# Gating tables made and applied ahead of the up tiles, not in a stage of their own

## The reference

```python
# peer(h, w_q, subkeys, u, v), per token; 8 heads, 16 experts each
# scores against two sets of 128 sub-keys, top 16 of each, top 16 of the sums
# -> per token 128 pairs (i1, i2) and gates g (softmax over a head's 16)
# hidden[e] = gelu(h . u[e])       for the experts picked, e = 128*i1 + i2
# y         = sum over picked e of  g * hidden[e] * v[e]
x = x + (g2[:, None, :] * y)
```

## Time and profile before

| | |
|---|---|
| median of 3 runs | 2908.99 us (2905.86 to 2910.26) |
| the profiled execution | 2908.07 us, span 2905.8 us from first to last instruction |
| mean granted TensorE clock | 0.983 |
| TensorE busy | 2771.0 us, 95% of the span |
| DVE, ACT, POOL busy | 1946.6, 1486.4, 1447.3 us |
| last up column to first down matmul | layer 0: 660.50 to 758.68 us; layer 1: 1711.12 to 1808.33 us |

### The profile page before, as it was taken

How to read it: one execution, slowest core, us unless ns; L and a number is a source line. 1 busy time by engine, 2 the same in 40 slices (tenths; PEclk the granted TensorE clock), 3 DMA queues, 4 the chain that set the end, 5 groups by cost and what they waited for, 6 DMA issues and landing times.

```text
span 2905.8 us, 53264 instructions
## 1 busy us (share of the span) xinstructions
PE 2771.0 (95%) x16662; PEld 2418.7 (83%) x16662; DVE 1946.6 (67%) x3521; ACT 1486.4 (51%) x2901; POOL 1447.3 (50%) x1137
## 2 busy tenths in 40 slices
PE   6999999997999999899999988999998999999998
PEld 6689999997777887789999986787878998876666
DVE  7736982338788887758940358888876544477776
ACT  1115554449645555455555568555545643255553
POOL 4831998888554441005989887544430000234442
PEclk8999999999999999899999999999999999999999
DMA  7634556770466663234555730766654533389994
GB/s 255 211 111 143 183 181 241 258 256 12 145 246 224 234 234 120 73 127 151 182 182 189 256 130 36 256 241 219 228 183 138 182 131 122 115 295 358 357 358 181
DMA packets 172454, 562.50 MB, mean 194 GB/s; under 512 B 15521, under 2 KB 18337, under 8 KB 172209
## 3 DMA queue, kind: packets, MB, share of 16 engines
q1 hardware_dynamic: 169968, 556.86, 54.6%
q10 hardware_dynamic: 2368, 4.19, 0.4%
HBM read 559.94 MB, written 1.05 MB: 193 GB/s over the span
## 4 chain that ended last, share of the span: by engine, by line
PE 59%; issue 19%; POOL 10%; ACT 7%; DVE 3%; DMA 1%; POOLq 0%; ACTq 0%; DVEq 0%; SPq 0%
PE bank L1094 20%; PE bank L1124 10%; PE bank L828 7%; PE bank L1417 6%; PE bank L887 5%; PE bank L1438 4%; ACT hT L1670 4%; POOL w_parts L2846 3%; ACT hT L1666 1%; POOL mean L2911 1%; POOL hT L2911 1%; DMA ring<-stream 1%; POOL mean L2913 1%; POOL hT L2913 1%; ACT h_parts L1678 1%
## 5 line engine op out<-in xcount | busy, mean ns | idle before, releaser
L2846 POOL TENSOR_TENSOR w_parts<-ring,w_parts 128x512 fp32r<-128x512 f32 x512 | 661.1, 1307 | 411.3 <-ACT w_parts L1630 378.2
L1094 PE MATMUL bank<-h_parts,w_parts 128*128 128x256 f32 x6144 | 751.8, 284 | 8.4 <-POOL w_parts L2846 6.1
L1094 PEld LDWEIGHTS bank<-h_parts,w_parts 128*128 128x128 f32 x6144 | 743.2, 192 | 9.4 <-issue 4.8
L1630 ACT ACTIVATE w_parts<-ring 128x512 fp32r<-128x512 f32 x512 | 320.0, 631 | 346.3 <-PE bank L1094 283.4
L1124 PE MATMUL bank<-h_parts,a_parts 128*128 128x512 f32 x1536 | 366.4, 394 | 8.1 <-DVE a_parts L2436 8.1
L1124 PE MATMUL bank<-w_parts,a_parts 128*128 128x512 f32 x1536 | 372.1, 398 | 1.3 <-DVE a_parts L2436 1.2
L1124 PEld LDWEIGHTS bank<-h_parts,a_parts 128*128 128x128 f32 x1536 | 284.6, 188 | 83.7 <-DVE a_parts L2436 25.3
L1124 PEld LDWEIGHTS bank<-w_parts,a_parts 128*128 128x128 f32 x1536 | 286.1, 190 | 62.4 <-DVE a_parts L2436 3.5
L1695 ACT ACTIVATE a_parts<-arena 128x256 fp32r (+1 forms) x256 | 107.0, 418 | 367.0 <-PE bank L1124 365.1
L828 PE MATMUL bank<-h_parts,w_parts 128*128 128x256 f32 x2304 | 282.5, 285 | 4.1 <-DVE w_parts L2027 4.1
L828 PEld LDWEIGHTS bank<-h_parts,w_parts 128*128 128x128 f32 x2304 | 279.7, 193 | 5.1 <-issue 4.4
(11 more groups left out here) (401 smaller groups left out, 4528.2 us busy)
## 6 DMA issues: line engine op xcount, KB each, us to landing
ring<-stream SPq DMA_DIRECT2D x594, 512.0 KB, 3.3
arena<-stream SPq DMA_DIRECT2D x105, 1024.0 KB, 7.3
arena<-stream SPq DMA_DIRECT2D x144, 512.0 KB, 4.5
hT<-stream SPq DMA_DIRECT2D x80, 512.0 KB, 4.4
mean<-stream SPq DMA_DIRECT2D x32, 512.0 KB, 4.5
arena<-consts ACTq DMA_DIRECT2D x1, 1536.0 KB, 6.5
xT<-xin ACTq DMA_DIRECT2D x1, 1024.0 KB, 10.7
out<-hT SPq DMA_DIRECT2D x4, 256.0 KB, 2.2
```

The costliest lines, as they stand in the source:

```text
L1094: mm = pe.matmul(bank[k][:, 0:T], w[:, wp, ws], h_parts[:, hp, 4 * j + q, :], start=(j == 0 and q == 0 and i == 0), stop=(j == 1 and q == ...
L1630: act.activation(w_parts[half % HALVES][:, 0, :], ring[slot_][:, j * 512:(j + 1) * 512], ACT.Copy).then_inc(sem(f"{n}_high"), 1)
L2846: pool.tensor_tensor(w[:, 1, :], ring[(base + k) % RING][:, j * 512:(j + 1) * 512], w[:, 0, :].bitcast(F32), ALU.subtract).then_inc(sem(f" ...
```

## The change

There is no table stage. A table group is four tokens, 64 groups in all, and group g is handled with up tile 64 + g (`TABLE_TILE` = 64). In order, for each step:

- DVE makes the four rows of `hot1` by one TENSOR_SCALAR per token (compare `iota`, copied to PSUM bank 6, with the first index, multiply by the gate; both are scalars per partition read from `route`), and `hot2` of the group by one TENSOR_TENSOR. `hot1` lies in the upper half of `hT`, `hot2` in `a_parts`, two groups each.
- TensorE runs the four table matmuls into bank 4 or 5 before the tile's 24 matmuls.
- DVE multiplies the table of group g-1 into all of `W` for its four tokens. For tiles whose gelu isn't there yet `W` holds ones, written by ACT (32 tiles, in its up tiles 56 to 63) and by a DVE memset (32 tiles).
- ACT's gelu of tiles 64 to 127 writes back into the tile's own bank, and DVE multiplies the bank into `W` (`gate_tile`), two steps later. TensorE writes the bank again when that is done.
- The modulation rows are summed by the same steps: one of the eight instructions after each `hot1` row. SP loads a row in two halves of 256 KB, each behind the ring load of one tile.

ACT's and POOL's parts of the one-hot work go away. Layer 0 has modulation rows in all 64 steps, layer 1 in its last 32.

```diff
+GROUP = 4
+GROUPS = T // GROUP
+TABLE_TILE = NK - GROUPS
...
+        hot1 = hT[:, 4:8, :].rearrange("p s (k n) -> p (s k) n", k=2)
+        hot2 = a_parts[:, :, :, :].rearrange("p x a t -> p (x a t)").rearrange("p (s n) -> p s n", n=P)
...
+                with sp.Fori(0, UP_ROWS // 2 - 1) as it:
+                    for k in range(4):
+                        r, i = k // 2, k % 2
+                        slots(it, RING + k, RING + k + 1)
+                        sp.wait_ge(sem("up_made" if i else "up_half"), it * 2 + (done + 2 + r))
+                        sp.dma_start(up_buffer(i), stream[it * 6 + (row + 3 * (2 + r)), :, i * 512:(i + 1) * 512])\
+                          .then_inc(up_landed[i], 16)
...
                 for c in range(RING):
                     sp.wait_ge(sem(f"{n}_low"), 2 * (NK - RING + c + 1))
-                    if c == RING - 1:
-
-                        sp.wait_ge(sem(f"{n}_table_free"), GROUPS + T // 4)
-                    v_load(c)
+                    v_load(c, False)
+                sp.wait_ge(sem(f"{n}_applied"), GROUPS + 2)
+                mod_load(seg, seg[0])
...
+            up_pe(pe, l, ROUTE_TILE, TABLE_TILE)
...
+            pe.sem_inc(sem(f"{n}_tabled"), 2)
+            for half in range(2):
+                first = TABLE_TILE + NK // 4 * half
+                up_pe(pe, l, first, first + NK // 4, rows=(first - UP_FROM[l]) // (2 * UP_ROWS) if first >= UP_FROM[l] else None,
+                      tables=GROUPS // 2 * half)
...
+        def table_pe(pe, n, it, k, first):
+
+            pe.wait_ge(sem(f"{n}_hots"), it * 4 + (first + k + 1))
+            pe.wait_ge(sem(f"{n}_applied"), it * 4 + (first + k + 1))
+            for s in range(GROUP):
+                slot_ = GROUP * (k % 2) + s
+                mm = pe.matmul(bank[4 + k % 2][:, s * P:(s + 1) * P], hot2[:, slot_, :].bitcast(F32), hot1[:, slot_, :],
+                               start=True, stop=True)
+            mm.then_inc(sem(f"{n}_tabled"), 1)
...
                 for k in range(4):
+                    if tables is not None:
+                        table_pe(pe, n, it, k, tables)
+                        pe.wait_ge(sem(f"{n}_gated_tile"), it * 4 + (tables + k + 1))
...
             for b in range(4, 8):
-
+                if b == 7:
+                    pe.wait_ge(sem("up_rows"), l + 1)
...
+            for i in range(ROUTE_TILE, TABLE_TILE):
+                gelu(slice(i, i + 1), i % 4, 2 * (i + 1))
+                if i == ROUTE_TILE:
+                    act.wait_ge(sem("turned"), TT * (l + 1))
+                at = TABLE_TILE + 4 * (i - ROUTE_TILE)
+                act.activation(W[:, at:at + 4, :].rearrange("p i (h n) -> p (i h) n", n=P), ones.unsqueeze(1).broadcast_to([P, 8, P]),
+                               ACT.Copy).then_inc(sem(f"{n}_ones"), 1)
+                high((i + 3) % 8, 2 * (i + 3), tile_at(i + 3), base)
+            with act.Fori(TABLE_TILE // 8, NK // 8 - 1) as it:
+                for k in range(8):
+                    gelu(None, k % 4, it * 16 + 2 * (k + 1), bank[k % 4][:, 0:T])
...
-                    act.wait_ge(sem(f"{n}_table_free"), GROUPS + T // 4)
+                    act.wait_ge(sem(f"{n}_applied"), GROUPS + 2)
+                if k == 1:
+                    act.wait_ge(sem(f"{n}_gated_tile"), GROUPS + 4)
...
+            iota_p = bank[6][:, T:T + P]
+            dve.tensor_copy(iota_p, iota).then_inc(signal("dve_step"), 1)
+            dve.memset(W[:, TABLE_TILE + NK // 4:NK, :], 1.0).then_inc(signal("dve_step"), 1)
...
+            def make_hots(first, it, k, tokens):
+
+                at = it * 16 + GROUP * (first + k)
+                if tokens[0] == 0:
+                    dve.wait_ge(sem(f"{n}_tabled"), it * 4 + (first + k + 1))
+                for s in tokens:
+                    dve.tensor_scalar(hot1[:, GROUP * (k % 2) + s, :], iota_p, route[:, 0, bass.ds(at + s, 1)],
+                                      route[:, 2, bass.ds(at + s, 1)], ALU.is_equal, ALU.mult)
+                    row_step(first, it, k, s)
...
+            def apply_table(first, it, k):
+
+                dve.wait_ge(sem(f"{n}_tabled"), it * 4 + (first + k + 3))
+                dve.wait_ge(sem(f"{n}_gated_tile"), it * 4 + (first + k + 3))
+                part = W[:, :, bass.ds(it * 16 + GROUP * (first + k), GROUP)]
+                dve.tensor_tensor(part, part, bank[4 + k % 2][:, :].rearrange("p (t i) -> p i t", t=GROUP), ALU.mult)\
+                   .then_inc(sem(f"{n}_applied"), 1)
+
+            def gate_tile(first, it, k, last=0):
+
+                dve.wait_ge(sem(f"{n}_applied"), it * 4 + (first + k + 4 - last))
+                dve.wait_ge(sem(f"{n}_gelu"), it * 4 + (TABLE_TILE + first + k + 1))
+                part = W[:, bass.ds(it * 4 + (TABLE_TILE + first + k), 1), :].rearrange("p i t -> p (i t)")
+                dve.tensor_tensor(part, part, bank[k % 4][:, 0:T], ALU.mult).then_inc(sem(f"{n}_gated_tile"), 1)
+
+            def step(first, it, k, skip=False):
+
+                make_hots(first, it, k, (0, 1))
+                if skip and k == 1:
+                    dve.wait_ge(sem(f"{n}_ones"), TABLE_TILE - ROUTE_TILE)
+                if not skip or k >= 1:
+                    apply_table(first, it, k - 1)
+                make_hots(first, it, k, (2, 3))
+                finish_hots(first, it, k)
+                if not skip or k >= 2:
+                    gate_tile(first, it, k - 2)
...
-            pool.wait_ge(sem(f"{n}_route"), TT)
-
-            with pool.Fori(0, T // TURN) as it:
```

More of the change, by code:

```diff
@@ L1079, in peer_pe, with up_pe @@
             back_pe(pe, n, "kv" if l == 0 else "mid", {0: ((act_y, 1), (dve_y, 1)), 2: ((act_y, 2), (dve_y, 2))})
-        def up_pe(pe, l, first, last, rows=None):
+        def table_pe(pe, n, it, k, first):
[6 more added lines that the diff above has]
+            mm.then_inc(sem(f"{n}_tabled"), 1)
+        def up_pe(pe, l, first, last, rows=None, tables=None):
             n = f"p{l}"
@@ L1631, in high, with gelu @@
                                    ACT.Copy).then_inc(sem(f"{n}_high"), 1)
-            def gelu(i, k, count):
+            def gelu(i, k, count, out=None):
                 act.wait_ge(sem(f"{n}_half_free"), HALVES + count)
-                act.activation(W[:, i, :], bank[k][:, 0:T], ACT.Gelu).then_inc(sem(f"{n}_gelu"), 1)
+                act.activation(W[:, i, :] if out is None else out, bank[k][:, 0:T], ACT.Gelu).then_inc(sem(f"{n}_gelu"), 1)
             def tile_at(i):
@@ L1647, in peer_act @@
             high(2, 4, tile_at(2), base)
-            for first, last in ((0, ROUTE_TILE), (ROUTE_TILE, NK - 8)):
-                if first:
-                    act.wait_ge(sem(f"{n}_picked"), TT)
-                with act.Fori(first // 8, last // 8) as it:
-                    for k in range(8):
-                        gelu(bass.ds(it * 8 + k, 1), k % 4, it * 16 + 2 * (k + 1))
-                        high((k + 3) % 8, it * 16 + 2 * (k + 3), it * 32 + tile_at(k + 3), base)
+            with act.Fori(0, ROUTE_TILE // 8) as it:
+                for k in range(8):
+                    gelu(bass.ds(it * 8 + k, 1), k % 4, it * 16 + 2 * (k + 1))
+                    high((k + 3) % 8, it * 16 + 2 * (k + 3), it * 32 + tile_at(k + 3), base)
@@ new lines, in up_row_dve @@
+            r = row % 2
+            total = bank[6][:, r * P:(r + 1) * P]
+            at = lambda n, per: it * (2 * per) + ((done + row) * per + n)
+            w = up_buffer(j // 4)[:, j % 4 * P:(j % 4 + 1) * P]
+            if j % 4 == 0:
+                dve.wait_ge(up_landed[j // 4], at(16, 16))
+            if j == 0:
+                dve.tensor_scalar(total, w, c[:, 0:1], None, ALU.mult).then_inc(sem("up_step"), 1)
+                return
+            if j == 4:
+                dve.wait_ge(sem("up_half"), at(1, 1))
+            else:
+                dve.wait_ge(sem("up_step"), at(j if j < 4 else j - 1, 6))
@@ L2260, in up_mods_dve, with up_rows_dve @@
+            if j == 7:
+                dve.wait_ge(sem("up_column"), at(1, 1))
+            out = up_part(r) if j == 7 else total
+            dve.scalar_tensor_tensor(out, w, c[:, j:j + 1], total, ALU.mult, ALU.add)\
+               .then_inc(sem({3: "up_half", 7: "up_made"}.get(j, "up_step")), 1)
+        def up_rows_dve(dve, l):
             dve.wait_ge(sem("up_column"), UP_DONE[l + 1] + 2)
             for n, (lo, hi) in enumerate(MODS_UP[l]):
-                dve.tensor_tensor(modv[:, lo:hi], bank[7][:, UP_ROWS * n:UP_ROWS * (n + 1)], V("mod_b")[:, lo:hi], ALU.add)\
-                   .then_inc(signal("dve_step"), 1)
@@ L2264, in up_mods_dve @@
[L2264 removed]
+                ins = dve.tensor_tensor(modv[:, lo:hi], bank[7][:, UP_ROWS * n:UP_ROWS * (n + 1)], V("mod_b")[:, lo:hi], ALU.add)
+            ins.then_inc(sem("up_rows"), 1)
+            dve.wait_ge(sem("up_rows"), l + 1)
         def peer_dve(dve, l):
@@ new lines, in peer_dve @@
+            for k in range(4):
+                step(0, 0, k, True)
```

(9 more changed lines are left out.)

176 lines of the change are left out of this document (35 added, 141 removed).

## The result

The changed kernel takes 2831.49 us (median of 4 runs, 2830.2 to 2835.67) against 2907.43 us: ratio 0.9741, 95% interval 0.9724 to 0.9758, some 76 us less. A second set of 5 runs gave 2831.4 us and 0.9737 (0.9715 to 0.9759). The forecast was 2851 us with a range of 2828 to 2889: the direction and the mechanism hold, but the gain was put at 57.6 us and is 76. The profiled execution has a span of 2828.1 us, 77.7 less than before's.

The account below looks back on a forecast made before the run. One-hot making bound the table stage, TensorE the stages around it. 96 x 4.06 + 32 x 3.85 + 2 x 4.5 - 2 = 520.0 us replaces 577.6, 57.6 less: 2851 us, range 2828 to 2889.

Parts of the forecast that it names:

- The stage was bound by making one-hots, and TensorE waited in it: Gating-table stage before down, 98.2 and 97.2 us: ACT and DVE busy 96 to 98% making one-hot rows, TensorE 78%.
- A group of table matmuls, 0.97 us: TensorE's cost for four tokens' table matmuls between up tiles, taken as 0.97 us between 0.89 and 1.13.
- A plain step: An up tile with its table group but no modulation row: 2.88 + 0.97 = 3.85 us, for 32 steps.
- The 0.1 us for what three near bounds cost each other: Added to TensorE's 3.96 us because DVE and the hand-off are close: 4.06 us per step with a modulation row.
- DVE's step, 3.73 us (3.60 to 3.85): DVE's start-to-start sum in a step with a modulation row; stays below TensorE's 3.96 us by 0.2 us.
- the second pointer: Second pointer scalar in DVE's one-hot row operations: costs 0 to 61 ns, so 0.29 us taken per row.
- POOL doesn't slow the steps: POOL's weight splitting beside DVE's new operations: nothing charged, as all but the memset have an input in PSUM.
- the ends: After each layer's last up tile, until the first down matmul: 4.5 us per layer.
- The clock credit of 2 us: Start of down: low clock after the stage with TensorE 78% busy costs 2.4 + 1.6 us; half credited.
- ACT's ones, DVE's memset, SP's half rows at nothing: Side work in and ahead of the up tiles: hidden or done in time, so no time charged.
- the one in which everything fits under TensorE: Rival: steps of 3.88 and 3.77 us, group at 0.89, clock stays high (4 us credit): 2829 us; chance 0.11.
- DVE-bound steps: Rival: DVE overhead makes the 96 steps with a modulation row 4.35 us, 27.8 us less: 2881 us; chance 0.25.

## Why the prediction was right, and where it was off

- **The stage was bound by making one-hots, and TensorE waited in it.** Right: TensorE's own need there was 55 of 91 us per layer, and most of the rest is the gain. Half its matmuls left out of the old stage gained nothing, though at a lower clock.
- **A group of table matmuls, 0.97 us.** Mis-sized: 0.83 and 0.90 in turn; what a group adds to a plain tile is 3.76 - 2.88 = 0.88, the lower bound of 0.89 from the weight loads. The 0.141 per record of the old stage had waits in it. A plain step came to 3.76 us against 3.85: 32 x 0.09 = 2.9 us.
- **The 0.1 us for what three near bounds cost each other.** This is the term that failed. Nothing of it was found: the step is 3.885 us, TensorE's own sum, with DVE at 3.83 beside it, and taking 0.5 us off DVE's part shortens it by less than 0.01. The allowance makes 9.6 us; with the cheaper group the 96 steps differ by 96 x 0.175 = 16.8 us.
- **DVE's step, 3.73 us (3.60 to 3.85).** The rows of before gave every term right but the second pointer, which lay at its upper end: 3.83. No time went to semaphore waits or register addresses between its instructions, but for the 0.10 us that it waits for TensorE in every second step. The room was 0.05 us; one operation more cost it all.
- **POOL doesn't slow the steps.** Right in the steps: row sums 343 ns in the mean while POOL was busy 66% of layer 0's. But the ends were mis-sized: 5.7 us per layer, not 4.5, as DVE's first down splits ran beside POOL's first row, which began behind them before (758.90). In layer 1 the slower clears would have held it at 5.3 us even without POOL. The Trainium skill (SBUF — State Buffer, Who interferes with whom) has just this case, two SBUF inputs against a GpSimd operation that reads SBUF; the trace agrees, with 2.99 us against 1.28. In the prediction I asked it only of the new operations. 2.4 us in all.
- **The clock credit of 2 us.** Wrong in its cause: in the changed kernel the clock at the start of down fell because of the clears of one row. The kernel before has the same clears, and was not run with full ones, so that they did it there too is likely and not shown. 0.7 us of the 4 came back (8.17 + 7.31 against 7.18 + 7.56).
- **ACT's ones, DVE's memset, SP's half rows at nothing.** Right. The memset took 6.88 us, from 443.67, and was long done at tile 64. Transfers made no wait.
- **Rivals.** What happened is the one in which everything fits under TensorE: 3.88 and 3.77 us a step and 2829 us; it had 0.11. Its clock credit of 4 us was wrong, but the stretch that the change leaves alone came out 5.8 us shorter in this profile. DVE-bound steps, given 0.25, were 0.05 us away. That the measured time still lies in the range is owed in part to luck: its lower end came from a rival that was right in the steps, with a clock credit of 4 us where 0.7 came back.

Sum of the terms: 57.6 + 16.8 + 2.9 - 2.4 - 1.3 = 73.6 us, where the trace has 577.6 - 504.5 = 73.1 in the stretches and 0.7 by the clock.

## What to carry to other kernels

A stage in which one engine of the next stage waits is worth the waiting only: count what that engine must still do, and put it between its other work. Count the others by starts, not durations, one engine at a time, and take the largest sum as the step; where buffers are two deep, sums a few hundredths of a microsecond apart did not add to each other here. When a stage disappears, look at what its end used to keep apart: here POOL's first row and DVE's first splits met.

## What was not expected of the hardware

- Table matmuls at half their number lowered the granted clock of the old stage from 1.00 to 0.68, so that they took almost as long as all of them.
- In and after clears on one row of the array the granted clock was 0.50, the level of 1.2 GHz, from 1727 to 1731 us; the same columns on 128 rows kept it at 1.00, through a wait of 1.88 us after them.
- The second pointer scalar of a TENSOR_SCALAR of 128 costs 58 ns: 344 ns with one, 402 with two.
- A DVE operation of 512 with two inputs in SBUF took 685 ns in POOL's pauses and 980 when it began beside a POOL operation.
- Two row sums of 128 in a chain take 0.65 us back to back; with a row between them, 0.26 each.
